# Order of the twelve thousand split-float products of the dense layers: by thirds of the tokens, or by weights

## The reference: what is computed

```
# layer 0: state-space heads beside latent attention
z = rmsnorm(x) @ e_w_in            # 1024 -> 1184 (padded to 1280)
x = x + concat(y_s5, o) @ e_w_out  # 1536 -> 1024
# layer 1: sliding-window attention
z = rmsnorm(x) @ o_w_in            # 1024 -> 1536
x = x + o @ o_w_out                # 1024 -> 1024
# after each of them: gated MLP, width 2816
g = h @ w_gate ; u = h @ w_up
c = conv_b + sum_j conv_w[j] * shifted(g, j)
x = x + (gelu(c) * u) @ w_down     # 2816 -> 1024
```

## Time and profile before

| | |
|---|---|
| median of 3 runs | 3704.56 us (3704.08 to 3706.44) |
| profiled execution, its own time | 3702.57 us |
| its span, first to last instruction | 3700.7 us |
| mean granted TensorE clock | 0.950 |
| TensorE products busy | 3273.6 us, 88% of the span, 22069 instructions |
| weight loads busy | 2868.6 us, 78%, 22069 |
| VectorE / ScalarE / GpSimd busy | 1704.2 / 703.9 / 886.0 us |

### The profile page before, as it was taken

How to read it: one execution, slowest core, us unless ns; L and a number is a source line. 1 busy time by engine, 2 the same in 40 slices (tenths; PEclk the granted TensorE clock), 3 DMA queues, 4 the chain that set the end, 5 groups by cost and what they waited for, 6 DMA issues and landing times. The chain is left out here.

```text
span 3700.7 us, 59460 instructions
## 1 busy us (share of the span) xinstructions
PE 3273.6 (88%) x22069; PEld 2868.6 (78%) x22069; DVE 1704.2 (46%) x2733; ACT 703.9 (19%) x1445; POOL 886.0 (24%) x490
## 2 busy tenths in 40 slices
PE   8746788888888886999999999997988999999997
PEld 7633466666766666989999999894548899999996
DVE  2296355455455553164352534315662552525252
ACT  2011133333233331031010000201540210101001
POOL 3100000000011103244443334332003344433431
PEclk9868899999899997999999999997989999999998
DMA  2000100100276652011111111111111111111111
GB/s 94 12 13 14 50 1 12 35 0 0 78 201 195 192 152 91 23 53 43 51 43 51 37 54 38 43 34 53 46 40 40 48 43 47 45 47 43 48 40 62
DMA packets 125928, 205.16 MB, mean 55 GB/s; under 512 B 14641, under 2 KB 92593, under 8 KB 125138
## 3 DMA queue, kind: packets, MB, share of 16 engines
q1 hardware_dynamic: 124690, 199.87, 17.7%
q10 hardware_dynamic: 1152, 4.23, 0.3%
HBM read 189.67 MB, written 6.25 MB: 53 GB/s over the span
## 5 line engine op out<-in xcount | busy, mean ns | idle before, releaser
L133 PE MATMUL ps_ffn_out<-sb_h_hi,sb_slab_hi_ffn 128*128 128x344 f32 x2112 | 675.0, 320 | 13.9 <-DVE sb_z L546 9.4
L134 PE MATMUL ps_ffn_out<-sb_h_hi,sb_slab_lo_ffn 128*128 128x344 f32 x2112 | 673.0, 319 | 0.0
L135 PE MATMUL ps_ffn_out<-sb_h_lo,sb_slab_hi_ffn 128*128 128x344 f32 x2112 | 672.7, 319 | 0.0
L115 POOL TENSOR_TENSOR sb_slab_hi_ffn<-sb_slab_raw,sb_ones 128x1024 fp32r<-128x1024 f32 (+2 forms) x152 | 256.7, 1689 | 927.6 <-PE ps_ffn_out L135 890.7
L133 PEld LDWEIGHTS ps_ffn_out<-sb_h_hi,sb_slab_hi_ffn 128*128 128x128 f32 x2112 | 396.3, 188 | 16.6 <-issue 16.6
L134 PEld LDWEIGHTS ps_ffn_out<-sb_h_hi,sb_slab_lo_ffn 128*128 128x128 f32 x2112 | 396.4, 188 | 0.0
L135 PEld LDWEIGHTS ps_ffn_out<-sb_h_lo,sb_slab_hi_ffn 128*128 128x128 f32 x2112 | 396.3, 188 | 0.0
L117 POOL TENSOR_TENSOR sb_slab_lo_ffn<-sb_slab_raw,sb_slab_hi_ffn 128x1024 fp32r<-128x1024 f32 (+2 forms) x152 | 359.7, 2367 | 11.9
L133 PE MATMUL ps_ffn_out<-sb_ffn_a_hi,sb_slab_hi_ffn 128*128 128x344 f32 x1056 | 336.7, 319 | 4.1 <-DVEq L540 4.1
L135 PE MATMUL ps_ffn_out<-sb_ffn_a_lo,sb_slab_hi_ffn 128*128 128x344 f32 x1056 | 337.9, 320 | 0.0
L134 PE MATMUL ps_ffn_out<-sb_ffn_a_hi,sb_slab_lo_ffn 128*128 128x344 f32 x1056 | 336.2, 318 | 0.0
(11 more groups left out here) (391 smaller groups left out, 5883.5 us busy)
## 6 DMA issues: line engine op xcount, KB each, us to landing
sb_dec_ck<-cache SPq DMA_DIRECT2D x512, 144.0 KB, 2.4
sb_slab_raw<-f_w_gu SPq DMA_DIRECT2D x88, 512.0 KB, 3.2
sb_slab_raw<-f_w_down SPq DMA_DIRECT2D x32, 384.0 KB, 3.1
sb_slab_raw<-f_w_down SPq DMA_DIRECT2D x32, 320.0 KB, 2.9
sb_slab_raw<-o_w_in SPq DMA_DIRECT2D x12, 512.0 KB, 3.2
sb_slab_raw<-e_w_in SPq DMA_DIRECT2D x10, 512.0 KB, 3.6
x_first<-x SPq DMA_DIRECT2D x8, 516.0 KB, 6.5
sb_z<-x ACTq DMA_DIRECT2D x8, 516.0 KB, 7.3
```

Source lines behind the costliest of these rows:

```text
L115: nc.gpsimd.tensor_tensor(hi, raw, one, ALU.mult).then_inc(self.hi_done[s], 1)
L133: nc.tensor.matmul(out(t), a, x_hi(k)[:, cols], start=start and k == 0, stop=False)
L134: nc.tensor.matmul(out(t), b, x_hi(k)[:, cols], start=False, stop=False)
L135: last = nc.tensor.matmul(out(t), a, x_lo(k)[:, cols], start=False, stop=stop and k == kc - 1)
```

## The change

Within a chunk the nine products come in another order. Before, each third of the tokens had its three products in a row, all into that third's bank, while the weights went hi, lo, hi. Now the hi weights take the three thirds of the hi tokens, then the three thirds of the lo tokens, and last the lo weights take the three thirds of the hi tokens; each product goes into another bank than the one ahead of it. The sums of a bank are the same nine terms per chunk, in another order. The first product into a bank (`start`) stays hi by hi; the last of a slab, which raises `mm_done`, is now lo weights by hi tokens.

```diff
             a, b = self.hi[:, s, k, :], self.lo[:, s, k, :]
+            cols = [slice(t * TT, (t + 1) * TT) for t in range(3)]
             for t in range(3):
-                cols = slice(t * TT, (t + 1) * TT)
-                nc.tensor.matmul(out(t), a, x_hi(k)[:, cols], start=start and k == 0, stop=False)
-                nc.tensor.matmul(out(t), b, x_hi(k)[:, cols], start=False, stop=False)
-                last = nc.tensor.matmul(out(t), a, x_lo(k)[:, cols], start=False, stop=stop and k == kc - 1)
+                nc.tensor.matmul(out(t), a, x_hi(k)[:, cols[t]], start=start and k == 0, stop=False)
+            for t in range(3):
+                nc.tensor.matmul(out(t), a, x_lo(k)[:, cols[t]], start=False, stop=False)
+            for t in range(3):
+                last = nc.tensor.matmul(out(t), b, x_hi(k)[:, cols[t]], start=False, stop=stop and k == kc - 1)
         last.then_inc(self.mm_done[s], 1)
```

## The result

The changed kernel is slower: 3723.77 us as the median of 5 runs (3719.91 to 3729.05), against 3704.56 us, the median of 5 runs (3701.81 to 3711.80), for the kernel before. The ratio is 1.005, with a 95% interval of 1.0035 to 1.0065, which is 13 to 24 us. The forecast of no change, 3692 to 3713 us, didn't hold it.

The account below looks back on a forecast made before the run. TensorE's distance between product starts, 156.5 ns over 12,528 dense products, was taken as the bound. Weights, bank and token terms were each 0, so 0 us on 3702.6 us, forecast as 3704.5 us, range 3692 to 3713.

Parts of the forecast that it names:

- The forecast of no change: Whole kernel: 0 us on the profiled 3702.6 us, 3704.5 us forecast, no effect given a chance of 0.80.
- What bounds the kernel: Dense stretches: only the distance between two products' starts sets the time, 156.5 ns each, 12.5 us per ns.
- The price of the kept weights: Dense products: weights kept on 5 of 9 products more (6960), 0 to -90 us, taken as 0.
- The one hint: Slab's start: a load alone takes at most 0.11 us, but 0.16 us pass from load to product.
- the excess of 13.0 ns: Each dense product at 2.4 GHz: time above the array's own 143.5 ns, 163 us in all, cause unnamed.
- The price of the bank: Dense products: bank changes on 6 of 9 products more (8352), -8 to +8 us, taken as 0.
- changing the bank costs: Rival, dense products: each bank change costs time, +8.4 us at 1 ns, 3713 us; slower given 0.07.
- The slab starts: Starts of slabs: the change leaves their waits as they are, 70 us in all.
- the price of the tokens: Dense products: token tile changes on 3 of 9 more (4176), -4 to +4 us, taken as 0.
- list of three things that differ: Per nine products: weights stay 7 times (before 2), bank changes 9 (before 3), token tile changes 9 (before 6).
- The bound of 1 ns per step: Dense products: rows of the three lines agree within 1 ns, applied to bank and token changes only.
- slower: Whole kernel: bank or token steps lose over 0.6 ns per product, chance 0.07.

Follow-up runs that it names:

- e1: Alternate slabs: changed kernel's tokens and banks with the earlier kernel's weights order, 157.84 ns per product; changed weights with earlier tokens and banks, 156.74 (gate and up).
- e3: Alternate slabs: changed token order with the earlier kernel's weights and banks, 157.84 ns per product; changed weights and banks with earlier tokens, 156.74 (gate and up).
- e6: Kernel before or changed order with other token widths, 64 weight columns or one weight tile: 118.19 ns (256 columns) to 232.36 (512); 156.68 and 156.70 for the weights.
- e2: Alternate slabs: changed banks with the earlier kernel's weights and tokens, 156.74 ns per product; changed weights and tokens with earlier banks, 157.84 (gate and up).
- e10: Third order, hi by hi, hi weights by lo tokens, lo by hi within each third, against the kernel before: 3709.05 us against 3706.06, ratio 1.0011.
- e5: Other token orders against both kernels' orders: hi, lo, hi of each third 156.71 ns per product; all tiles at the weights' place 157.78 in both orders.
- e7: Changed kernel's order, all tiles at one start place, weights' slabs elsewhere in memory: 155.50 to 160.00 ns per product by distance; some slabs 153.33.

## Why the prediction was wrong

**What bounds the kernel** was right: the distance of two products' starts sets the time, and one ns per product is 12.5 us. It was this sensitivity that decided, since the result hangs on 0.8% of a step.

**The price of the kept weights**, 0, was right: the table of e1 to e3 shows 0.1 ns at most, and e6 shows that nothing was to be had: with one weight tile for all nine, or half the weight columns, the step stays at 156.7. The 22069 loads stayed, as the earlier trace rows had led one to expect. The one hint that the excess of 13.0 ns had to do with the load led nowhere: the excess stays when the load is halved, and it is another at other widths.

**The price of the bank**, 0, was right (e2, e3). The rival "changing the bank costs" came nearest in time, 3713 us at 1 ns against 3723.77 measured, by a mechanism that e2 refutes: with the new banks and the old row of tokens the step is 156.74.

**The slab starts** kept their 70 us, as forecast.

**The step that failed is the price of the tokens**: "3 of 9 (4176), 1 ns either way: -4 to +4 us; I take 0". It measured 12.8 us. Over 4176 products that would be 3.1 ns each, and the count is wrong too: of the 70 steps of a gate or up slab behind its first one, 52 moved by more than 1 ns, up as well as down, and not only those where the tile's change is new. In the durations this can't be seen: in the changed kernel the three lines, each with another kind of step behind it, still last alike, in 100 us of the MLP (count, busy, mean ns, idle; the busy times are small because a group's overlapping records are counted once):

```profile
L135 PE MATMUL ps_ffn_out<-sb_h_lo,sb_slab_hi_ffn 128*128 128x344 f32 x213 | 45.2, 320 | 0.0
L137 PE MATMUL ps_ffn_out<-sb_h_hi,sb_slab_lo_ffn 128*128 128x344 f32 x212 | 44.8, 319 | 0.0
L133 PE MATMUL ps_ffn_out<-sb_h_hi,sb_slab_hi_ffn 128*128 128x344 f32 x210 | 44.5, 320 | 0.0
```

And the price isn't one of a tile's change. The prediction's list of three things that differ lacks a fourth, the row of places that the tiles start at. The earlier trace rows were read as if each of the three kinds of step paid its own price, so that equal rows meant equal prices. They can't show that, since the price of another order stands in no row of this one. Nor were the steps equal: by the starts in all gate and up slabs of before they are 157.2 ns behind L133, 156.9 behind L134 and 155.9 behind L135, 1.3 ns apart where the durations differ by 0.9. It is a price of neither bank nor tile: e2's old row of tokens with new banks has 157.1, 157.0 and 156.0, and e10, with other products second and third, 157.2, 156.9 and 156.0. e5 shows it from both sides: hi, lo, hi changes the tile at each product and costs nothing, and with all places equal the new order costs nothing against the old one. In the large stretches what counts is the whole row of places at which the tiles start, within 256 bytes.

The bound of 1 ns per step was about right in size (+1.2 and -0.8), but it should have stood on every product: 12,528 times 1 ns either way gives -12.5 to +12.5 us about 3704.5. Even that ends at 3717, short of 3723.77, but it holds nearly all of the 12.8 us of the steps, and it asks for a chance of "slower" above 0.07.

**What stays open.** Why a row of places gives its step: neither a sum of places nor their distance from the weights alone foretells it, one place has two or three values, and in small slabs the slab ahead seems to count. And the 4.5 us of the 17.3 between the two profiles that the steps don't hold, most of which lie in time at the lower clock. The interval of 13 to 24 us begins just where the 12.8 us of the steps end, while e10's 3.0 us agree with its 3.4 us of steps; so a part of the rest may belong to the change by a way that no run shows.

## What to carry to other kernels

When an order of products is changed, the addresses that it streams from come in another order too; before weights and banks get the credit or the blame, give each its own run, with the other two held. Equal durations of all kinds of step in one trace say nothing on the price of another order: bound such a price on every product, not on the changed ones. Where steps differ within a slab and come back in the same places, look for what repeats with their period. A step's mean over a slab, read from the same product in two consecutive slabs, shows a difference of 0.1 ns where the duration of a line rounds it away.

## What the runs showed of the hardware

- fp32r products of 128 by 128 weights don't follow one another at a column per cycle at the upper clock (e6): 118.19 ns for 256 columns, 146.58 for 320, 173.34 for 384 and 232.36 for 512 are 11.5 to 19.0 ns more than the columns at 2.4 GHz. At the lower clock show no such excess.
- Within a slab of the kernel before single steps go from 151.7 to 160.9 ns and repeat after 24 products, as the row of start places within 256 bytes does.
- With all tiles at one place the step of one and the same row of instructions goes from 154.9 to 160.0 ns, mostly with that place (e7), and three slabs took 153.33.
- In gate and up a change of the PSUM bank at every product, 6 products with the same weights, and 64 instead of 128 weight columns each change the step by 0.1 ns at most.
- The stretch between w_in and w_out's state-space part, with the same instructions in thirteen traces, took 1261.4 to 1270.7 us, 227.5 to 254.3 of them at the lower clock.
